# Shifting the slots of HH and HL, and the blocks of TH, by 32 bytes each in an fp32r transformer kernel

## What is computed

```python
h = h + concat(gla(n), mla(n)) @ w_out
h = h + square(relu(rms_norm(h) @ w_mlp_up)) @ w_mlp_down      # 1024 -> 4096 -> 1024
h = h + (p @ w_ple_proj) * sigmoid(rms_norm(h) @ w_ple_gate + b)
for i in (0, 1):                                               # second block
    x = x + (pool_mixer(h) if i == 0 else chunk_attention(h))
    x = x + (silu(conv3(h @ w_gate)) * (h @ w_val)) @ w_out    # 1024 -> 2816 -> 1024
```

## Time and profile before

| | us | share of the span |
|---|---|---|
| median of the runs | 1630.73 | |
| span of the profiled execution | 1630.0 | 100% |
| TensorE busy (matmuls) | 1623.6 | 100% |
| weight loads, beside the matmuls | 1345.9 | 83% |
| VectorE busy | 1017.8 | 62% |
| ScalarE busy | 660.2 | 41% |
| GpSimd busy | 115.0 | 7% |

### The profile page before, as it was taken

The page is one execution under the profiler, slowest core; times in us unless marked ns, Lnnn a source line. Parts: engine busy times, 40 slices in busy tenths (PEclk is TensorE's granted clock), DMA queues, the critical chain, the costliest instruction groups (busy, mean ns, idle before and its releaser), DMA issues.

```text
span 1630.0 us, 20189 instructions
## 1 busy us (share of the span) xinstructions
PE 1623.6 (100%) x8480; PEld 1345.9 (83%) x8480; DVE 1017.8 (62%) x1523; ACT 660.2 (41%) x919; POOL 115.0 (7%) x102
## 2 busy tenths in 40 slices
PE   9999999999999999999999999999999999999999
PEld 7877878898989888888888888877777888888887
DVE  6797664696756757576466357546655576366353
ACT  5476445354444446333122223456565333122221
POOL 1300000011111100000000000312101100000000
PEclk9999999999999999999999999999999999999999
DMA  5310228356454521222322313322221223222211
GB/s 187 109 46 27 104 78 121 82 115 136 87 135 86 161 84 72 79 102 104 107 100 100 107 59 124 101 94 87 76 77 52 78 104 111 98 102 98 109 59 71
DMA packets 28059, 156.01 MB, mean 96 GB/s; under 512 B 3712, under 2 KB 5392, under 8 KB 12096
## 3 DMA queue, kind: packets, MB, share of 16 engines
q1 hardware_dynamic: 26352, 149.75, 25.7%
q0 software_dynamic: 1328, 4.86, 5.5%
q10 hardware_dynamic: 288, 0.10, 0.0%
HBM read 149.98 MB, written 4.72 MB: 95 GB/s over the span
## 4 chain that ended last, share of the span: by engine, by line
PE 94%; DVE 3%; ACT 2%; DMA 1%; POOL 0%; issue 0%; SPq 0%; DVEq 0%; ACTq 0%
PE bank L725 23%; PE bank L726 23%; PE bank L727 23%; PE bank L731 3%; PE bank L733 3%; PE bank L732 3%; PE bank L1183 2%; PE bank L1185 2%; PE bank L1184 2%; PE bank L1421 1%; PE bank L980 1%; PE bank L1431 1%; PE bank L1447 1%; ACT WH L1490 1%; DMA RAW<-in_W 1%; PE bank L965 1%
## 5 line engine op out<-in xcount | busy, mean ns | idle before, releaser
L1913 DVE TENSOR_TENSOR WL<-RAW,WH 128x2048 fp32r<-128x2048 f32 (+2 forms) x122 | 273.0, 2243 | 193.5 <-ACT WH L1490 193.5
L725 PE MATMUL bank<-AH,WH 128*128 128x512 f32 (+1 forms) x974 | 382.9, 393 | 0.6 <-DVE WL L1963 0.4
L727 PE MATMUL bank<-AH,WL 128*128 128x512 f32 (+1 forms) x974 | 379.2, 389 | 0.0
L726 PE MATMUL bank<-AL,WH 128*128 128x512 f32 (+1 forms) x974 | 379.1, 389 | 0.0
L1490 ACT ACTIVATE WH<-RAW 128x2048 fp32r<-128x2048 f32 (+2 forms) x122 | 227.0, 1867 | 174.3 <-PE bank L727 138.0
L725 PE MATMUL bank<-HH,WH 128*128 128x512 f32 x608 | 236.6, 389 | 0.0
L726 PE MATMUL bank<-HL,WH 128*128 128x512 f32 x608 | 236.6, 389 | 0.0
L727 PE MATMUL bank<-HH,WL 128*128 128x512 f32 x608 | 236.5, 389 | 0.0
L725 PEld LDWEIGHTS bank<-AH,WH 128*128 128x128 f32 (+1 forms) x974 | 182.5, 187 | 42.4 <-issue 2.4
L727 PEld LDWEIGHTS bank<-AH,WL 128*128 128x128 f32 (+1 forms) x974 | 182.4, 187 | 38.7
L726 PEld LDWEIGHTS bank<-AL,WH 128*128 128x128 f32 (+1 forms) x974 | 182.5, 187 | 38.3 <-issue 1.0
(11 more groups left out here) (347 smaller groups left out, 2378.9 us busy)
## 6 DMA issues: line engine op xcount, KB each, us to landing
RAW<-in_W SPq DMA_DIRECT2D x124, 1024.0 KB, 4.8
RAW<-in_W SPq DMA_DIRECT2D x9, 768.0 KB, 4.2
X<-in_XT SPq DMA_DIRECT2D x16, 256.0 KB, 5.4
ev_scratch<-ev POOLq DMA_DIRECT2D x16, 160.0 KB, 7.6
Gb<-ev_scratch SPq DMA_DIRECT2D x16, 128.0 KB, 3.0
Gb<-ev_scratch SPq DMA_DIRECT2D x16, 112.0 KB, 2.7
out<-X SPq DMA_DIRECT2D x7, 256.0 KB, 2.0
RAW<-in_W SPq DMA_DIRECT2D x2, 512.0 KB, 5.6
```

Source lines behind the costliest of these rows:

```text
L725: e.matmul(o, a, h, start=first, stop=False)
L726: e.matmul(o, a, l, start=False, stop=False)
L727: return e.matmul(o, c, h, start=False, stop=last)
L1913: e.tensor_tensor(k.WL[j][:, 0:n], k.RAW[RAW_OF[u]][:, 0:n], k.WH[j][:, 0:n].bitcast(F), SUB).then_inc(*WLO.mark(u))
```

## The change

HH0 to HH9 and HL0 to HL4 get 32 bytes of distance after each, so their starts are 2080 bytes apart; HL5 to HL9 follow without. Counted from the region's start (256 modulo 512), HH[s] then lies at 32 s (0 to 288), HL[0] to HL[4] at 320, 352, 384, 416 and 448, HL[5] to HL[9] at 448, all modulo 512. In the code the distances after HH0 to HH9 and after HL0 to HL3 are the 14 that are added. The blocks of TH get 264 instead of 256 elements of room, so they start 1056 bytes apart; counted from an address of 256 modulo 512, block (c, kind) lies at 32 (3 c + kind), 0 to 352, and every block of TL at 384. The buffers that share memory with these (band, xg, G, YZ) move along. The views of TH are cut to 0:256. No instruction is added or removed.

```diff
-    k.HH = [a.tile(f"HH{i}", [P, S], R) for i in range(NH)]
-    k.HL = [a.tile(f"HL{i}", [P, S], R) for i in range(NH)]
+    k.HH, k.HL = [], []
+    for i in range(NH):
+        k.HH.append(a.tile(f"HH{i}", [P, S], R))
+        a.at += 32
+    for i in range(NH):
+        k.HL.append(a.tile(f"HL{i}", [P, S], R))
+        a.at += 32 if i < 4 else 0
...
-    a.at += 192
-    shapes_at = inner + 192
-    k.TH = a.over("TH", [P, 4, 3, 256], shapes_at, R)
-    k.TL = a.over("TL", [P, 4, 3, 256], shapes_at + 4 * 12 * 256, R)
-    k.xg = a.over("xg", [P, 2, S], shapes_at + 4 * 24 * 256)
-    k.G = a.over("G", [P, S], shapes_at + 4 * 24 * 256)
-    k.YZ = a.over("YZ", [P, 2, 256], shapes_at + 4 * 24 * 256 + 4 * S)
+    a.at += 384
+    k.TH = a.over("TH", [P, 4, 3, 264], inner, R)
+    k.TL = a.over("TL", [P, 4, 3, 256], inner + 4 * 12 * 264, R)
+    inner_end = inner + 4 * 12 * 520
+    k.xg = a.over("xg", [P, 2, S], inner_end)
+    k.G = a.over("G", [P, S], inner_end)
+    k.YZ = a.over("YZ", [P, 2, 256], inner_end + 4 * S)
...
-              enumerate([base + 4 * S * 8] + [base + 4 * S * (NH + 8) + 4 * 4 * BW * i for i in range(3)])]
+              enumerate([base + 8 * (4 * S + 32)] + [base + NH * (4 * S + 32) + 4 * (4 * S + 32) + 4 * 4 * S + 4 * 4 * BW * i for i in range(3)])]
...
-                h, lo = (z[:, c, "dce".index(x), :] for z in (k.TH, k.TL))
+                h, lo = (z[:, c, "dce".index(x), 0:256] for z in (k.TH, k.TL))
```

More of the change, by code:

```diff
@@ L1734, in scalar_program @@
             w.wait_ge(DVE("t2", c), MM("unit", UNIT["up", FIRST_FAST - 1]))
-            e.activation(k.TH[:, c, 0:2, :], k.stage[:, 0, :].rearrange("p (i n) -> p i n", i=2), AF.Copy).then_inc(*ACT.mark("th", c, 0))
+            e.activation(k.TH[:, c, 0:2, 0:256], k.stage[:, 0, :].rearrange("p (i n) -> p i n", i=2), AF.Copy).then_inc(*ACT.mark("th", c, 0))
             w.wait_ge(DVE("t4", c))
-            e.activation(k.TH[:, c, 2, :], k.stage[:, 1, 0:256], AF.Copy).then_inc(*ACT.mark("th", c, 1))
+            e.activation(k.TH[:, c, 2, 0:256], k.stage[:, 1, 0:256], AF.Copy).then_inc(*ACT.mark("th", c, 1))
             e.activation(AH[:, c, 256:512], k.stage[:, 1, 256:512], AF.Copy).then_inc(*ACT.mark("th", c, 2))
@@ L2394, in shapes @@
         w.wait_ge(ACT("th", c, 2))
-        e.tensor_tensor(k.TL[:, c, 0:2, :], k.stage[:, 0, :].rearrange("p (i n) -> p i n", i=2), k.TH[:, c, 0:2, :].bitcast(F), SUB)
-        e.tensor_tensor(k.TL[:, c, 2, :], t3, k.TH[:, c, 2, :].bitcast(F), SUB)
+        e.tensor_tensor(k.TL[:, c, 0:2, :], k.stage[:, 0, :].rearrange("p (i n) -> p i n", i=2), k.TH[:, c, 0:2, 0:256].bitcast(F), SUB)
+        e.tensor_tensor(k.TL[:, c, 2, :], t3, k.TH[:, c, 2, 0:256].bitcast(F), SUB)
         e.tensor_tensor(AL[:, c, 256:512], t4, AH[:, c, 256:512].bitcast(F), SUB).then_inc(*DVE.mark("tl", c))
```

## The result

The changed kernel takes 1642.78 us (median of 2 runs, 1641.83 and 1643.72) against 1630.73: ratio 1.0076, 95% interval 1.0055 to 1.0098. It is 12 us slower, where +7.9 was forecast, in the forecast's direction and inside its range.

The account below looks back on a forecast made before the run. The prediction took TensorE's distances between matmul starts to bound the kernel. Profiled span 1630.0 + 6.1 (HH and HL) + 1.8 (TH and TL) = 1637.9, with 0.7 from span to median 1638.6 us; range 1618 to 1645.

Parts of the forecast that it names:

- What bounds the kernel: TensorE, busy over the whole span at full granted clock, waits some 3 us together; only distances between matmul starts matter.
- HH and HL, +3.3 ns, +6.1 us: 1824 matmuls with HH or HL as moving operands go from 226.7 to an unsettled 230.0 ns each.
- nine to settle: On TensorE, after a change, distances between matmul starts take about nine matmuls to reach one settled value.
- no two successive matmuls read at the same place: In the shifted HH and HL triples, places always change, so distances never settle; +3.3 ns on each of 1824 matmuls.
- lock: On TensorE, operands all at the same place modulo 512 make matmuls repeat one settled distance; 226.7 ns at 512 columns.
- The bounds: HH and HL: 220.0 to 233.3 ns each, -12.2 to +12.2 us; TH and TL: -1.3 to +2.6 us.
- TH and TL, +1.8 us: 396 fast-form matmuls of 256 columns go from 113.3 to an unsettled 117.8 ns, +4.5 ns each.
- The pool mixer, band, and the other engines at 0: 96 mixer and 64 band matmuls, at most 0.6 and 0.4 us, taken as 0; VectorE, ScalarE, GpSimd stay hidden, 0.
- Rival A: HH and HL matmuls: spreading beats offset 0, losing part of 13.3 ns excess; 1622 us (1617 to 1628), chance 0.32.
- B: TensorE's distances: wandering offsets average to the same 226.7 ns, nothing happens; 1630.7 us (1629 to 1632), chance 0.14.
- C: HH and HL matmuls: each 6.7 to 13.3 ns over, worse than unsettled; 1645.5 to 1657.6 us, chance 0.10.
- The rule on read ports: TensorE's independent ports for moving operand and weights: no address could change a distance, 1630.7 us; the prediction doubted it.

Follow-up runs that it names:

- the run of the part alone: Only the shifts of HH, HL and band, TH and TL as in the kernel before: 1641.07 us beside 1629.21, ratio 1.0067.
- the list: Mean ns per 512-column matmul, kernel before changed to put each stage's HH and HL slots at one place modulo 256; three kernels: 1639.01, 1636.96, 1645.98 us.
- the runs alone: Only the wider blocks of TH and TL, HH and HL as in the kernel before: 1632.14 us, ratio 1.0015.

## Why the prediction was right or wrong

- *What bounds the kernel*: right, but for "at full granted clock throughout" (the 3.5 us above). No engine and no wait took part; TensorE's waits are the same few and its distances carry all of it.
- *HH and HL, +3.3 ns, +6.1 us*: the mis-sized term. Measured +6.0 ns, +10.9 us by the distances, 11.9 by the run of the part alone (8 to 13 by its interval). The size came from a mean over nine matmuls after a change, of which only the first five were unsettled. The sixth starts here:

```profile
378.73 0.39 PE L727 MATMUL bank<-HH,WL 128*128 128x512 f32 x1
```

378.73 - 377.57 is 1.16 us, 232 ns each for the first five, and 227 for the other four. The kernel after has no single distance, and its mean stays near 232.7. Nor is "nine to settle" general: the changes that the earlier trace rows show are of width or place. In the kernel before, HH triples that follow AH triples (same width, same place) take 226.7 from the first on; in the kernel with all slots at 192 those that follow AH triples take 233.3 from the first on.
- *The cause given, "no two successive matmuls read at the same place"*: the step that failed, though the number came out in range. All slots alike at 192, with no unequal neighbours, cost 12.1 us in the profile, more than the spread's 10.9: the slots left the one good place, and that alone is dear. Weighed by how often each is read, the settled prices of the list for the changed kernel's places give 232.0 to 232.4 ns (with 229.0 to 233.3 for 64), for 232.7 measured; this is a sum and not a measured split, since with mixed places the list isn't the whole price. (In the code eight pairs of the last group of down products do read one slot twice running, which is too few to matter.) Unequal neighbours were shown to cost by themselves where some of the operands stand at the good place (HH at 0, HL at 64 or 32); a mixture of bad places alone was not run against the list. That the sign came out right is therefore in part luck: a lock that any equal place restores would have made the kernel with 192 as fast as before.
- *The bounds*: the upper one for HH, 233.3, held. The low one, 220.0, was carried over from 256 columns to 512 and has no place in the list. A place that is better at one width (113.3 for 120.0) is worse at the other (233.3 for 226.7).
- *TH and TL, +1.8 us*: right in size, +1.6 by the distances, 2.9 (1 to 4 by the interval) by the runs alone.
- *The pool mixer, band, and the other engines at 0*: right. From start to start the mixer's 96 matmuls on HH together, and the 64 of band together, changed by less than 0.1 us between the profiles.
- *Rival A (spreading is faster)* fell; *B* fell with the interval; *C* (the worst on every matmul, 233.3, and TH at its bound) at 1645.5 or more is just above the measured 1642.8. Its price was nearer to the truth than mine for HH: the first three distances of the transient, 233.3 on average, which I took for an upper bound, equal the settled price of most places.
- *The rule on read ports* (the Trainium skill, SBUF — State Buffer, "Who interferes with whom": TensorE has two independent read ports and never waits on anyone) gave 1630.7. These runs don't agree with it taken as "addresses don't matter": moving the weights by 320 bytes, with AH and AL left where they were and the start addresses of HH and HL unchanged modulo 512, cost 34 us. The two streams concerned are both TensorE's own; the section is about ports that engines share, and says nothing of addresses.

No version here beats the kernel before; the two that shift everything alike equal it. Why the offset to the weights sets the distance was not shown.

## What to carry to other kernels

Where TensorE runs gapless on fp32r products, compare the distance of matmul starts with the columns over the clock, and vary the start of the moving operand against that of the weights: here 0 modulo 256 bytes gave 226.7 ns for 512 columns and every other multiple of 32 gave 229 to 234. Keep all moving operands at the one good offset, not only most of them, since one in three off place took the value from the others (227.4 by the list, 232 measured). Test each width by itself, and don't take a settled price from a transient.

## What the runs showed of the hardware that was not expected

- At 2.4 GHz the settled 226.7, 233.3, 113.3 and 120.0 ns are 544, 560, 272 and 288 cycles, all multiples of 16. Where the single distances differ, as for AH at 192 with the weights moved (231 and 236 in turn), two of them together are 466.7 ns, 1120 cycles, again a multiple of 16. What inside the chip has that step was not shown.
- One place can have two settled values: 113.3 or 117.8 ns at 192 and 256 columns, 228.9 or 233.3 at 64 and 512 columns, there according to what ran ahead.
- Offsets of 256 bytes are equal to none, and moving all tiles by 64 or 128 bytes has no effect (ratio 1.0002 each).
